# Two transformer blocks on one core: moving twelve modulation tiles from a feed-forward loop into an attention, and reordering the second layer

## The reference

```python
cond = silu(c)
for i in range(4):
    mod = cond @ ada_w[i] + ada_b[i]                  # 1024 x 6144
    sh_a, sc_a, g_a, sh_f, sc_f, g_f = split(mod, 6)
    h = modulate(rms_norm(x, g[i, 0]), sh_a, sc_a)
    y = mixer_i(h)
    x = x + g_a * rms_norm(y, g[i, 1])
    h = modulate(rms_norm(x, g[i, 2]), sh_f, sc_f)
    y = square(relu(h @ ffn_w1[i])) @ ffn_w2[i]
    x = x + g_f * rms_norm(y, g[i, 3])
```

```python
q = rope(rms_norm(p_q)); k = rope(rms_norm(p_k)); v = p_v    # k, v: 512 tokens
o = (softmax(q0 @ k0.T / 8) - lam * softmax(q1 @ k1.T / 8)) @ v   # 4 heads
y_hy = gate_out * (irfft(rfft(gate_in * val) * rfft(filter)) + bias * (gate_in * val))
```

## Time and profile before

| what | value |
|---|---|
| runs | 3088.41, 3100.31, 3095.72 us |
| median | 3095.72 us |
| profiled execution, its time | 3100.6 us |
| its span, first to last instruction | 3098.6 us |
| mean granted clock of TensorE | 0.958 |
| TensorE busy | 2767.5 us (89%) |
| VectorE busy | 1166.5 us (38%) |
| ScalarE busy | 933.1 us (30%) |
| DMA | 796.20 MB, mean 257 GB/s |

### The profile page before, as it was taken

One profiled execution on the slowest core, in us unless ns is written; L12 is line 12 of the kernel. 1 busy time (PEld: TensorE's weight loads), 2 busy tenths in 40 slices (PEclk: granted clock), 3 DMA queues, 4 the chain that ended last, 5 costly groups with the idle time before them and its releaser, 6 DMA issues.

```text
span 3098.6 us, 35159 instructions
## 1 busy us (share of the span) xinstructions
PE 2767.5 (89%) x13676; PEld 1746.3 (56%) x13676; DVE 1166.5 (38%) x2100; ACT 933.1 (30%) x1680; POOL 39.4 (1%) x51
## 2 busy tenths in 40 slices
PE   8999877777889888777789999998999999999899
PEld 3443422222564452222245788857888988875787
DVE  1752200002331320000134544446676465443766
ACT  2112211011212320000024444545445454443543
POOL 0010000000000000000000000000000000000000
PEclk9999999999999999999998999999999999998999
DMA  7673599999612859999960566672546525662152
GB/s 331 264 313 130 222 427 429 428 429 429 288 60 82 326 221 428 429 428 429 429 274 1 230 265 264 247 303 98 190 161 239 189 87 232 282 258 99 54 189 97
DMA packets 59497, 796.20 MB, mean 257 GB/s; under 512 B 8637, under 2 KB 9917, under 8 KB 10749
## 3 DMA queue, kind: packets, MB, share of 16 engines
q1 hardware_dynamic: 55664, 790.13, 61.8%
q10 hardware_dynamic: 3724, 4.59, 0.4%
HBM read 793.64 MB, written 1.05 MB: 256 GB/s over the span
## 4 chain that ended last, share of the span: by engine, by line
PE 70%; DMA 20%; DVE 5%; ACT 3%; issue 2%; SPq 0%; ACTq 0%; DVEq 0%; POOL 0%; POOLq 0%
DMA ring<-in_t_up 11%; PE banks L1925 11%; PE banks L1485 6%; PE banks L917 5%; PE banks L1949 5%; DMA ring<-in_t_down 5%; PE banks L785 5%; PE banks L932 4%; PE banks L1360 4%; PE banks L1942 4%; DMA ring<-in_t_gate 3%; PE banks L1501 3%; PE banks L754 3%; PE banks L1945 2%; PE banks L774 1%
## 5 line engine op out<-in xcount | busy, mean ns | idle before, releaser
L1485 PE MATMUL banks<-ring,arena 128*64 128x512 f32 x1792 | 419.5, 623 | 104.4 <-DMA ring<-in_t_up 56.3
L2947 DVE TENSOR_TENSOR ring_lo<-ring,w_hi 128x1024 fp32r<-128x1024 f32 x256 | 312.6, 1225 | 289.3 <-ACT w_hi L2342 288.7
L2342 ACT CAST w_hi<-ring 128x1024 fp32r<-128x1024 f32 x256 | 267.9, 1053 | 404.2 <-PE banks L1925 199.0
L1485 PEld LDWEIGHTS banks<-ring,arena 128*64 128x64 f32 x1792 | 148.4, 143 | 373.6 <-issue 355.6
L2529 DVE TENSOR_TENSOR arena<-arena,banks 128x512 f32<-128x512 f32 x32 | 22.0, 687 | 804.6 <-PE banks L1485 804.6
L2062 ACT COPY arena<-banks 32x512 f32 x96 | 55.3, 577 | 608.2 <-PE banks L1501 607.5
L1501 PE MATMUL banks<-ring,arena 128*64 128x512 f32 x896 | 205.2, 612 | 28.1 <-DMA ring<-in_t_down 16.9
L1925 PE MATMUL banks<-w_hi,ffn_h_hi 128*128 128x512 f32 x512 | 203.6, 398 | 0.0
L1925 PE MATMUL banks<-w_hi,ffn_h_lo 128*128 128x512 f32 x512 | 199.6, 390 | 0.0
L1925 PE MATMUL banks<-ring_lo,ffn_h_hi 128*128 128x512 f32 x512 | 199.6, 390 | 0.0
L1949 PE MATMUL banks<-u_pair,w_hi 128*128 128x256 f32 x1024 | 187.7, 285 | 2.4 <-DVE ring_lo L2947 2.1
(11 more groups left out here) (362 smaller groups left out, 4223.9 us busy)
## 6 DMA issues: line engine op xcount, KB each, us to landing
ring<-in_t_ada SPq DMA_DIRECT2D x72, 2048.0 KB, 8.6
ring<-in_t_ffn SPq DMA_DIRECT2D x64, 2048.0 KB, 11.8
ring<-in_t_gate SPq DMA_DIRECT2D x56, 2048.0 KB, 21.4
ring<-in_t_up SPq DMA_DIRECT2D x56, 2048.0 KB, 21.7
ring<-in_t_down SPq DMA_DIRECT2D x56, 2048.0 KB, 20.5
ring<-in_t_ret_in SPq DMA_DIRECT2D x12, 2048.0 KB, 8.3
arena<-in_t_gate SPq DMA_DIRECT2D x8, 2048.0 KB, 26.7
arena<-in_t_up SPq DMA_DIRECT2D x8, 2048.0 KB, 27.0
```

What stands on the lines that cost most here:

```text
L1485: mm = nc.tensor.matmul(PS[64 * h:64 * h + 64, f.bank, :], x_cur[:, b, k, :], wview(un[h0 + h], KC)[:, k, :], start=(k == 0), stop=(k == K ...
L2342: nc.scalar.copy(w_hi[:, n % 4], w).then_inc(S("ffn_w_hi"), 1)
L2947: TT(w_lo, w, w_hi[:, n % 4].bitcast(F32), ALU.subtract).then_inc(S("ffn_w_lo"), 1)
```

## The change

The plan, the three programs of b0's mixer and those of the second layer change. In the plan, b1's twelve tiles are loaded between b0's attention weights and its out weights, with all row products on bank 7 and all transposed tiles on bank 5. To free these two, b0's scores go round three banks instead of four, its value products have bank 4 alone, and so have its rotations. b0 leaves `ADA_IN_FFN` and enters `PAIRED`. Nothing changes for b3's mixer.

```diff
-            use_dense("qk_in", load(turn(2), units_of(a["t_in_cd"], 0, 1)), 4, [0, 1, 2, 3] * 2)
-            use_dense("v_in", load(turn(1), units_of(a["t_in_cd"], 2)), 4, [4, 5, 6, 7])
+            use_dense("qk_in", load(turn(2), units_of(a["t_in_cd"], 0, 1)), 4, [6, 7, 0, 1, 2, 3, 6, 7])
+            use_dense("v_in", load(turn(1), units_of(a["t_in_cd"], 2)), 4, [4, 5, 4, 5])
             fills("qk_ms", [0, 1, 2, 3] * 2)
-            fills("qk_rot", [4, 5, 6, 7] * 2)
+            fills("qk_rot", [6, 7, 6, 7, 0, 1, 2, 3])
...
-        ADA_IN_FFN = (0, 2)
-        PAIRED = (1, 3)
+        ADA_IN_FFN = (2,)
+        PAIRED = (0, 1, 3)
...
+                early = fills(p + "cols_early", [5] * 2) if i == 0 else []
...
-                fills(p + "qrot", [4, 5] * 2)
+                fills(p + "qrot", [4] * 4 if i == 0 else [4, 5] * 2)
...
-                fills(p + "scores", [0, 1, 6, 7] * 4)
+                fills(p + "scores", ([0, 1, 6] * 6)[:16] if i == 0 else [0, 1, 6, 7] * 4)
                 fills(p + "turn", [2, 3] * 8)
-                fills(p + "pv", [4, 5] * 4)
+                fills(p + "pv", [4] * 8 if i == 0 else [4, 5] * 4)
+                if i == 0:
+                    au = load(turn(12), units_of(a["t_ada"][i + 3], *range(12)))
+                    fr = fills(p + "ada_rows", [7] * 12)
+                    plan[p + "ada_cols"] = early + fills(p + "cols_late", [5] * 10)
...
# TensorE, second layer (qk_pe, qk_ms, qk_rot and value_tile hold the old bodies)
                 forward(plan["hy_ufreq"], hy_utok)
+                u_ready(pe, c, 1)
+                qk_pe(0, 2)
                 pe.wait_ge(S("hy_Y"), 4)
...
+                qk_pe(2, 8)
+                value_tile(0)
                 pe.wait_ge(S("da_const"), 16)
+                qk_ms(0, 4)
+                value_tile(1)
+                qk_rot(0, 2)
+                qk_ms(4, 8)
+                value_tile(2)
+                qk_rot(2, 8)
+                value_tile(3)
...
# TensorE, b0's mixer: tile_rows(n) is ada_rows_pe, tile_cols(n) is ada_cols_pe, both only for i == 0
+                tile_rows(0)
                 stat_pe(pe, c, 2, plan[p + "ms"][0], N)
                 stat_pe(pe, c, 1, plan[p + "ms"][1], N)
+                tile_rows(1)
...
+                tile_cols(0)
                 w = wview(us[1], 2)
...
+                tile_cols(1)
+                tile_rows(2)
+                tile_rows(3)
+                tile_cols(2)
                 pe.wait_ge(S("ml_rope"), 5 * (j + 1))
...
                     if s < 16:
                         scores(s)
+                    if s % 2 == 1 and s < 16:
+                        tile_rows(4 + s // 2)
+                    if s % 2 == 0 and s < 17:
+                        tile_cols(3 + s // 2)
...
# ScalarE, second layer
                 for t, f in enumerate(plan["v_in"]):
                     copy_act(act, f, da_v[:, t, :], PS[:, f.bank, :])
-                for i, f in enumerate(plan["qk_ms"]):
-                    rsqrt_act(act, c, f, N if i < 4 else 2 * N, 64, dst=da_rs[:, i, :])
+                    if t < 2:
+                        for i in range(4 * t, 4 * t + 4):
+                            rsqrt_act(act, c, plan["qk_ms"][i], N if i < 4 else 2 * N, 64, dst=da_rs[:, i, :])
...
# ScalarE, b0's mixer: tile_rows(n) is rows_act, from n = 4 on behind the transpose of tile n - 2;
# tile_rows(0) stands behind the squares, tile_rows(1) behind the key part's copy, 2 and 3 ahead of the loop
                 for s in range(1, 16 + 6):
                     if s <= 16:
                         exps(s - 1)
+                    if s % 2 == 1 and s < 16:
+                        tile_rows(4 + s // 2)
...
# VectorE, second layer (the bodies of the two old loops)
+                qk_norm(0, 4)
+                qk_rope(0, 2)
+                qk_norm(4, 8)
+                qk_rope(2, 8)
...
# VectorE, b0's mixer: tile 0 ahead of the rotations, 1 and 2 behind them, the rest in the loop
                     if s >= 2:
                         soft_b(s - 2)
+                    if s % 2 == 1:
+                        tile_cols(3 + s // 2)
```

More of the change, by code:

```diff
@@ L789, in dense_pe @@
                     between(i)
-        def token_pe(pe, name, tchunks):
-            units, fs = plan[name + "_units"], plan[name]
-            for i, u in enumerate(units):
-                w = wview(u, KC)
-                u.landed.wait(pe)
-                for t in range(tchunks):
-                    f = fs[i * tchunks + t]
-                    f.open(pe)
-                    for q in range(KC):
-                        mm = nc.tensor.matmul(PS[:, f.bank, :], uT[:, q, t * P:(t + 1) * P], w[:, q, :],
-                                              start=(q == 0), stop=(q == KC - 1))
-                    mm.then_inc(f.full.sem, 1)
         def quarter(p, n):
@@ L1589, in _, with qk_pe @@
                 forward(plan["hy_ufreq"], hy_utok)
+                u_ready(pe, c, 1)
+                def qk_pe(lo, hi):
+                    for n in range(lo, hi):
+                        u, f, width = plan["qk_in_units"][n // 4], plan["qk_in"][n], (N, 2 * N)[n // 4]
+                        w, m = wview(u, KC), n % 4
+                        if m == 0:
+                            u.landed.wait(pe)
+                        f.open(pe)
+                        for q in range(KC):
+                            mm = nc.tensor.matmul(PS[:, f.bank, 0:width], w[:, q, m * P:(m + 1) * P],
+                                                  uT[:, q, 0:width], start=(q == 0), stop=(q == KC - 1))
+                        mm.then_inc(f.full.sem, 1)
+                qk_pe(0, 2)
                 pe.wait_ge(S("hy_Y"), 4)
@@ new lines, in qk_ms, with qk_rot @@
+                def qk_ms(lo, hi):
+                    for i in range(lo, hi):
+                        f, width = plan["qk_ms"][i], N if i < 4 else 2 * N
+                        pe.wait_ge(S("qk_sq"), i + 1)
+                        f.open(pe)
+                        nc.tensor.matmul(PS[:, f.bank, 0:width], da_half, da_sq[:, i, 0:width], start=True, stop=True)\
+                            .then_inc(f.full.sem, 1)
+                def qk_rot(lo, hi):
+                    for i in range(lo, hi):
+                        f = plan["qk_rot"][i]
+                        pe.wait_ge(S("qk_n"), i + 1)
+                        f.open(pe)
+                        nc.tensor.matmul(PS[:, f.bank, 0:N], da_swap, da_qk[:, i, 0:N], start=True, stop=True)\
+                            .then_inc(f.full.sem, 1)
@@ new lines, in value_tile @@
+                def value_tile(t):
+                    u, f = plan["v_in_units"][0], plan["v_in"][t]
+                    w = wview(u, KC)
+                    if t == 0:
+                        u.landed.wait(pe)
+                    f.open(pe)
+                    for q in range(KC):
+                        mm = nc.tensor.matmul(PS[:, f.bank, :], uT[:, q, t * P:(t + 1) * P], w[:, q, :],
+                                              start=(q == 0), stop=(q == KC - 1))
+                    mm.then_inc(f.full.sem, 1)
```

76 lines of the change are left out of this document (41 added, 35 removed).

## The result

| | before | after |
|---|---|---|
| median of 5 runs each, same chip | 3093.95 us (3085.91 to 3100.31) | 3068.39 us (3065.35 to 3071.43) |
| ratio, with its 95% interval | | 0.9922 [0.9905, 0.9938] |
| the profiled execution | 3100.6 us (span 3098.6) | 3069.03 us (span 3067.0) |

What follows compares the result with a forecast made beforehand. The chain was 70% TensorE and 20% DMA, with no DMA in the touched stretches. Second layer -18.9, attention +16.4 and feed-forward -34.0 sum to -36.5 us, from the median 3095.72 to 3059 us; range 3044 to 3081.

Steps and rivals of the forecast that it cites:

- Second layer, -18.9: Second layer: reordered work fills TensorE's waits, first scores 17.9 us earlier, then 1.0 us less at full clock; -18.9 us.
- Does it survive the expert loop: Expert loop behind the second layer: its load-bound stretch moves with TensorE's chain, so the second layer's gain counts whole.
- The rival that said no: Expert loop: its loads hide the second layer's gain anyway; -17.6 us in all, 3078 us; chance 6%.
- Feed-forward, -34.0: b0's feed-forward: without three tiles per round and with the paired form, 8.50 us less in each of four rounds; -34.0 us.
- Four tiles ahead of the loop, +3: b0's attention before its loop: four tiles mostly fill TensorE's waits, the clock gives -1.5; +3 us, bounds -1 and +13.9.
- the last wait: Ahead of b0's first scores: two rows and two transposes fill a 4.02 us wait, with later rotations; +3.3 us.
- The loop, +13.4: b0's attention loop: remaining tiles at full clock, five new 0.75 us waits for ScalarE; 52.0 against 38.6 us, +13.4 us.
- SyncE's queue: b0's tile and weight loads: each lands ahead of its use; the constants' load taken as 0, at most 3.2 us.
- The loop stays at 1.2 GHz: Rival, b0's loop: pairs of 10.3 us at half clock, +30 us; sum -6.5, 3089 us; chance 7%.
- The tiles only move: Rival, b0: no wait takes any tile, so feed-forward's gain is gone; sum -18.9, 3077 us; chance 10%.
- Tiles one by one: Rival, b0's loop: each tile loads only after the one before is read, pairs of 11 us; +13, 3109 us; chance 4%.
- More than forecast: Rival, b0's attention: ScalarE's copies come early enough, loop 46 us, start at -1; -46.5, 3049 us; chance 15%.

Runs made afterwards that it cites:

- e4: Kernel after, but in the second layer only the two query products move ahead of the inverse transform, the rest in old order; one run, 3069.46 us.
- e1: Kernel before with only the second layer's new order, b0 as before; median 3076.05 us, ratio to before 0.9931.
- e3: Kernel after, but b0's feed-forward keeps the unpaired form, three instructions of 256 columns; one run, 3061.86 us.
- e12: Kernel after, but ScalarE issues the load of b0's constants ahead of the block instead of beside tile 3; one run, 3058.66 us.
- e6: Kernel after, but rows and transposes of tiles 1 to 3 go between b0's rotations; one run, 3062.73 us.
- e8: Kernel after with the edits of e6, e7 and e12 together; median 3056.57 us, ratio to before 0.9871.
- e10: The kernel of e8 again, on another chip; median 3053.44 us, ratio to before 0.9853.
- e7: Kernel after, but in b0's loop ScalarE copies the turned probabilities before the tile's rows; one run, 3065.34 us.
- e2: Kernel before with only b0's part of the change, second layer in its old order; median 3077.55 us, ratio to before 0.9937.
- e11: Kernel before run again without edit, as a control; median 3095.46 us, ratio to before 1.0004.
- e5: Kernel after run again without edit, on the second chip; median 3059.16 us, ratio to before 0.9872.
- e9: Kernel after run a third time without edit, on the third chip; median 3066.41 us, ratio to before 0.9901.

## Why the prediction came out as it did

The forecast of 3059 us lies 9.4 us under the first median and within its range. The stretches that the change touches, and what lies between them, give 27.4 us where 36.5 were forecast. The other 4.1 us of the profiles' 31.6 lie ahead of the second layer and behind b0, where nothing was forecast: that the profiled gain comes as near as it does is in part luck. It is point by point so:

- **Second layer, -18.9: right to the first scores, with 1.4 us for the rest instead of -1.0.** The starts of the inverse transform (906.3, or 907.3 with the 1.0 us by which everything began earlier; forecast 907.4) and of the scores (985.8 in the same way, forecast 985.5) are as worked out. What I had wrong is the sentence "They run at full clock then, 1.0 us less". The scores did, 1.99 against 3.78 us, but the wait for VectorE ahead of the first transposes grew from 0.28 to 2.12 us, and the half clock came 6.6 us behind the scores' start and hit a tile's rows. So the attention takes 0.6 us more than before (130.29 against 129.69) instead of 1.0 less. In e4, with the waits ahead of the scores, the fall comes ahead of them, 9.5 us; with the waits closed it comes behind. The other 0.8 us lie in the expert layer and are not explained.
- **Does it survive the expert loop: right**, by e1. The rival that said no (3078 us) is ruled out; its kernel would have had b0's norm where it was.
- **Feed-forward, -34.0: right** (-33.9). The next block's round was the right row. e3 adds what the row could not tell apart: the tiles are 8.05 and the pairing 0.40 us of a round.
- **Four tiles ahead of the loop, +3: mis-sized; it was +8.6**, inside the bounds of -1 and +13.9. Rows 0 cost nothing, as said (the wait of 2.89 became 1.92 of work and 1.15 of wait). Ahead of the query products it was +2.8, not +1.0. Rows 1 and the first transposes make the forecast 1.0 of it, and the constants' load 1.5, the term that I took as 0 with an end of 3.2. The rest are two terms of the clock that nearly cancel: from the first norm to the latent product it takes 1.2 us more, since 5.5 us behind the first norm are at half clock instead of 2.9, and the sums of squares and the key part take 1.0 less. So the clock's -1.5 was -1.6 in the query products and -1.0 ahead of them, less the 1.2; and that e12, without the wait for the load, measures 28.01 us, +1.0 as forecast, is luck in so far. The 1.2 us are no cost of the tiles: e1, with b0 as before, has them too (6.29 us from the first norm to the latent product, before 5.08), and e3 has not (5.07). The larger miss is the last wait, +7.4 for +3.3. The rotations take 8.52 us from the first to the transposes (1633.13 to 1641.65) and the two rows and two transposes 7.83 us to the scores (1649.48); forecast were 6.8 and 5.4. The durations account for it: two rotations at 1.93 instead of 1.04 us, one set of rows at 3.64 instead of 1.92, one of transposes at 1.11 instead of 0.66. The step that failed is "since TensorE no longer idles 4 us ahead of the loop" the half clock goes. It does leave the loop, but it stands ahead of it: with one bank the rotations became four pieces of work of 1.0 us with waits of 0.9 us between, and the clock fell in the middle of them. That these waits belong to the fall, e6, e8 and e10 show: with them filled the rotations run at full clock. And the trace of before could have warned. TensorE's timeline and windows of before at its rotations:

```profile
1652.98 1.04 PE L1737 MATMUL banks<-arena 64*64 64x512 f32 x2 [0.88 <-DVE arena L2787]
```
```profile
1654.02:1654.62 0.60, 0.00 (x1) 0.00 (x0) 0.60 (x2) 0.00 (x0) 0.00 (x0) 0.91 0.00 0
1654.62:1658.04 3.42, 0.00 (x0) 0.00 (x0) 3.30 (x6) 0.00 (x0) 0.00 (x0) 0.50 0.00 0
```

The last rotation ends at 1654.0, and at 1654.5 the clock falls. The wait of 4.02 us was 0.5 us old then, 57.5 us behind the first norm; after, the fall comes at 56.7. So the fall did not hang on the length of that wait, and filling it could not be expected to take the fall away. What made it last 23.9 us before and 10.2 after is not shown.

- **The loop, +13.4: right** (+14.1). The waits are 0.82 us where I had 0.75, in the place and for the reason given; e7 shows the reason. To the last scores it took 43.03 us (forecast 43.5), the tail 9.31 (8.5). Two of the tail's value products wait for ScalarE, 0.40 and 0.84 us, but that isn't the single bank: before, with two banks, the same two waited 0.47 and 0.84 us. The 1.6 us that the prediction takes for a wait of TensorE ahead of the first probabilities is a piece of VectorE on the chain (1665.6 to 1667.2), in which TensorE was at the next scores; nothing was to be had there, and the sum does not use it.
- **SyncE's queue: right.** All tiles landed ahead of their use. The median landing over the whole kernel went from 8.6 to 10.0 us.

**The rivals.** *The loop stays at 1.2 GHz* (3089 us) is wrong: 1.00 in every window of the loop. The rule of the Trainium skill ("TensorE: Matmul & The Clock Gate", section "A second HAM failure mode: psum-queue depth-cycling") would have had short idles swing the clock there. This trace doesn't agree for the loop, where 0.82 us of wait stood in every 6.54 us. At the rotations, where 0.9 us of wait stood in every 1.9 us, it shows one fall, but on a single bank and not going round several. *The tiles only move* (3077 us) fails on the same clock of 1.00 and on e2, which is faster by 0.6%. *Tiles one by one* (3109 us) fails on pairs of 6.54 us where it needed 11; it was not tried by itself. *More than forecast* had the loop at 46 us and the start at -1; neither came in the changed kernel, but e7 has a loop of 45.8 us (37.58 + 8.25), so its first half describes what another order on ScalarE would have brought.

**What stays open.** The upstream -1.0 us and the -3.1 us behind b0 are scatter and no gain: these stretches hold the same instructions, and the kernel before, profiled once more in e11, moves by more in the first (896.8 us against 893.4) and by as much in the last (b1 to the end 1142.4 us against 1145.8, where after has 1142.7). The end of the first expert loop scatters from 792.7 to 799.4 us over the 14 profiled executions, in kernels that do the same work up to there; why, no run shows. Nor can I say why the kernel after is 0.8% faster in the first comparison, 1.3% in the second and 1.0% in the third, where the first two intervals don't meet. The stretches that the change touches repeat to 0.1 us in after, e5 and e9 (92.38; 16.35; 43.03; 9.31), so it isn't in these. No run keeps two banks for the rotations while the tiles are there, so that the single bank makes their waits is read from the timeline (VectorE's line 2862 releases it) and not tried by itself.

## What to carry to other kernels

Work put into a wait is free only if the clock behind the wait stays as it was: read the granted clock on both sides of the place, and price what follows at 1.2 GHz once as an upper end. When a resource is taken away to free it for something else (here a bank of the rotations), write the instruction sequence out with the remaining one; a row of short pieces with waits as long as themselves costs more than the waits. And where two copies of one engine feed a busy one, the order of the two is worth a whole wait per step: e7 moved two lines and took back 6.5 us.

Before a wait is blamed for a low clock, look when the clock fell: in the trace of before it was down 0.5 us into a wait of 4.02 us, so the length of that wait was not its cause.

## What the runs showed of the hardware that was not expected

- A fall of the granted clock near b0's loop stood in every kernel, whichever wait was closed. It came 57.5 us behind the first norm before (23.9 us at 0.50), at 56.7 after (10.2 us), at 66.2 in e6 (3.4 us), at 63.1 in e8 and e10 (6.8 us). Its length also changes with no edit to b0's mixer: e3 has 6.8 us where after has 10.2.
- The 288 KB of constants, issued 0.7 us behind a 2048 KB tile, landed in 7.55 us; before, with no tile beside it, b0's load took 2.9 us, the quicker of the two; in e3 the same wait was 2.31 instead of 1.53 us.
- Whole times of one kernel on one chip scatter over 12 to 18 us (e9: 3054.69 to 3067.33; e10: 3040.58 to 3058.18), while most stretches repeat to 0.1 us where the clock's low pieces lie alike. Where they don't, a stretch moves too: rotations to scores take 16.35 us in after and 15.17 in e3, with the same instructions. An edit worth 3 us is read from its stretch, with the clock beside it, and not from the total.
